# Working each normalization of a two-block network in two parts of 256 tokens, with the slab of matmuls ahead of it and the group behind it taken part by part

## The chip, the cores and the metric

The kernel runs on one core of one Trainium2 chip. The metric is the device time of one execution in microseconds (us), lower is better. The core has engines that each run their own instruction stream in order and meet through semaphores: TensorE (PE in the profile; PEld is its loading of weights), VectorE (DVE), ScalarE (ACT), GpSimd (POOL), and SyncE (SP), which here only issues the transfers of weights.

## The reference, cut to what is computed

Two blocks of a transformer run one behind the other, each of two layers, on 256 latent tokens and 256 context tokens with 1024 features, all in float32. Every layer normalizes its tokens, modulates them with a shift and a scale that come from a product of a conditioning vector with a weight, multiplies them with wide weights and adds the result, times a gate, to the residual. The latent and the context tokens have tables of their own.

```python
def rms_norm(x, gain=None):
    xf = x.astype(jnp.float32)
    y = xf * lax.rsqrt(jnp.mean(xf * xf, axis=-1, keepdims=True) + EPS)
...
def modulate(h, shift, scale):
    return h * (1.0 + scale) + shift

def swiglu(h, w_in, w_out):
    gate, up = jnp.split(h @ w_in, 2, axis=-1)
    return (jax.nn.silu(gate) * up) @ w_out
...
    for l in range(DEPTH):
...
        m_lat = (silu_c @ w_mod[l] + b_mod[l]).reshape(Bsz, N_MOD, 1, D)
...
        x = x + 0.5 * m_lat[:, 2] * swiglu(modulate(rms_norm(x), m_lat[:, 0], m_lat[:, 1]), ffn_in[l, 0], ffn_out[l, 0])
...
        h_lat = modulate(rms_norm(x), m_lat[:, 3], m_lat[:, 4])
...
        x = x + m_lat[:, 5] * o_lat
        x = x + 0.5 * m_lat[:, 8] * swiglu(modulate(rms_norm(x), m_lat[:, 6], m_lat[:, 7]), ffn_in[l, 1], ffn_out[l, 1])
```

The first block has attention with a recurrent branch in its layer 0 and windowed attention in layer 1. The second block has, in each layer, a mixer of three branches and a feed-forward part with a short convolution, with the same kind of normalization and modulation in front of each.

## The kernel before

**Layout.** All activations are held with features on the 128 partitions: a tensor is 8 tiles of 128 features ("k-tiles") by 512 tokens, the 256 latent ones first, the 256 context ones behind them (`HALVES` holds the two ranges, `NT` is 512, `KD` is 8). `X` is the residual. `H` holds the normalized and modulated tokens, `HH` their rounded high part and `HL` the rest. Weights are taken apart the same way, so every product is three matmuls: high by high, high by low, low by high. All outputs of a group stand in PSUM banks, one bank of 512 columns for each 128 output features.

**Slabs.** Weights arrive in slabs of 1 MB (4 k-tiles by 512 output columns, so 4 x 4 x 3 = 48 matmuls; in the deep product 2 k-tiles by 1024, also 48). SyncE loads them into a ring of three buffers (`slab_in`, issued at L2036): a slab's transfer waits until the slab that was three earlier has been used up. A slab is *split* into its high part by ScalarE (L1197, recorded at L1189, `WR<-ring`) and then its low part by VectorE (recorded at L1486, `WR<-ring,WR`), into one of two pairs of buffers, so ScalarE's write waits for TensorE to be done with the slab two earlier.

**Normalizations.** There are 12: `nf00`, `ne`, `n2`, `nf10`, `no`, `n11` and `fin` in the first block, `nm0`, `nc0`, `nm1`, `nc1` and `gfin` in the second. `n11`, `nc1`, `fin` and `gfin` cover 256 tokens, the others 512. One goes in this order, over all its tokens at once: ScalarE squares each tile of X as soon as its last addition is made (`sq`); TensorE adds the squares over the features in two steps of four tiles (`sum`, the second behind tile 7); ScalarE copies the sums out, TensorE turns them to one column for 128 tokens (`rstd`), VectorE and ScalarE form the reciprocal root, TensorE spreads it over the partitions (`spread`). Then for each of the 8 k-tiles VectorE multiplies (`times`, `H<-X,bank`), ScalarE modulates, one instruction for each half of tokens (`mod_h`, `H<-H,MOD`), and for even tiles also writes the high part; VectorE writes it for odd tiles and subtracts the low part for all (`mod_l`, `HL<-H,HH`).

**Products.** `lin` makes a product with 8 k-tiles in groups of four outputs, two slabs a group. A group is usually taken output by output. Its first group behind a normalization is taken k-tile by k-tile (`slab_all`), so that it can start at the first low part. `lin_deep` is the product out of a feed-forward part: 22 k-tiles, 8 outputs, 11 slabs. Where a product ends a layer part, its last slab is followed, output by output, by the addition of the bank into X (`ev`, L1495, for 512 tokens one instruction for each half) and by the square.

**Modulation tables.** The tables are products of one column with a weight as large as a layer. Their slabs of 1 MB (`in_w_mod`, `in_w_ada`) go through the same ring, but are used unsplit: eight matmuls of 512 columns on them (`bank<-ring,silc`). They run as background work in the loops over slabs of certain feed-forward parts: `between()` is called behind every slab and lets through, at a rate, so many steps of a generator (1.5 a slab in `f00`, 1.9 in `2`, 1.3 in `f10` and `c0`); what is left over runs behind the loop, ahead of the deep product.

**What sets the order.** The program first makes one list, `ORDER`, by calling these functions; then each engine's program walks it and issues its own part. The splits are put in last, in the loop at L780 to L795: ahead of each slab those of all slabs up to one further on, and one at each `split_next`, which stands behind the low part of k-tile 4 of a normalization:

```python
            if step[0] == "slab_all" or step[0] == "slab" and step[3] == 0:
                n = SLABS[step[1].slabs[step[2]][0]]["n"]
                while todo and SLABS[todo[0]]["n"] <= n + 1 and SLABS[todo[0]]["split_from"] <= at_hold:
                    steps.append(("split", todo.pop(0)))
```

In the profile many instructions bear the line of a helper: matmuls L820, ScalarE's activations L1189, VectorE's operations of two tensors L1486, with a scalar L1490 and L1492, additions with a gate L1495, reciprocals L1501.

## Time and profile before

| | |
|---|---|
| median of 3 runs | 4165.21 us (4158.31 to 4174.64) |
| profiled execution | 4163.52 us |
| its span in the trace | 4161.7 us |
| TensorE matmuls busy | 3745.4 us, 90% of the span |
| VectorE, ScalarE, GpSimd busy | 47%, 33%, 2% |
| mean granted clock of TensorE | 0.938 of full |
| transfers | 453.74 MB, mean 109 GB/s |

TensorE is busy for nine tenths of the span, though "busy" holds overlaps: consecutive matmuls of the same kind are pipelined and their ends are modelled, so counts and starts tell more than the sum of busy times. The other engines are idle more than half of the time. The span is that of one profiled execution; the 1.8 us between it and the execution's time lie around it.

### The profile page before, as it was taken

How to read it: one execution, taken by the hardware profiler on the slowest of the kernel's cores; microseconds unless marked ns; L12 is line 12 of the kernel's file. 1: busy time of each engine (PE TensorE's matmuls, PEld its weight loads, DVE VectorE, ACT ScalarE, POOL GpSimd, SP SyncE). 2: the span in 40 equal slices, each digit the busy share in tenths (PEclk: the TensorE clock that was granted, in tenths of full speed). 3: DMA queues.
4: the chain of work that ended last, by engine and by line, in shares of the span. 5: the costliest groups of instructions: out<-in, count | busy, mean ns of one | idle time of the engine just before them, and what ended most of it. 6: DMA issues, size and time to landing. Idle time of an engine off the chain costs nothing.

```text
span 4161.7 us, 59269 instructions
## 1 busy us (share of the span) xinstructions
PE 3745.4 (90%) x25936; PEld 2992.4 (72%) x25936; DVE 1969.7 (47%) x3272; ACT 1369.4 (33%) x2089; POOL 75.1 (2%) x106
## 2 busy tenths in 40 slices
PE   7999978588869999999989997998999999998898
PEld 4778754587646777677765996666777778777898
DVE  2223365888852223323355553654434453464575
ACT  3113324233331122222233443333233232343453
POOL 0000001100000000000000000010000000010000
PEclk9999988799989999999975998999999999999999
DMA  6553212000025552454220552121224442222453
GB/s 248 207 192 112 71 33 18 4 3 3 3 81 212 201 191 93 143 180 162 91 71 10 163 182 91 52 66 46 72 91 152 161 166 98 91 86 81 145 165 122
DMA packets 257906, 453.74 MB, mean 109 GB/s; under 512 B 14096, under 2 KB 157584, under 8 KB 243184
## 3 DMA queue, kind: packets, MB, share of 16 engines
q1 hardware_dynamic: 253840, 441.68, 31.2%
q0 software_dynamic: 3808, 8.27, 1.2%
q8 instruction: 204, 3.34, 0.3%
q14 instruction: 54, 0.44, 0.0%
HBM read 447.24 MB, written 1.94 MB: 108 GB/s over the span
## 4 chain that ended last, share of the span: by engine, by line
PE 73%; DVE 15%; ACT 7%; DMA 3%; issue 1%; POOL 0%; SPq 0%; DVEq 0%; ACTq 0%; POOLq 0%
PE bank L820 71%; DVE WR L1486 3%; ACT WR L1189 2%; DMA ring<-in_ffn_in 2%; ACT W L1189 2%; PE bank L991 2%; DVE W L1495 2%; DVE HF L1486 2%; DVE W L1501 1%; DVE W L1486 1%; DVE HF L1495 1%; ACT H L1189 1%; DVE H L1486 1%; DVE X L1495 1%; ACT HH L1189 1%
## 5 line engine op out<-in xcount | busy, mean ns | idle before, releaser
L820 PE MATMUL bank<-HH,WR 128*128 128x512 f32 (+1 forms) x8736 | 2401.0, 360 | 124.1 <-DVE WR L1486 71.9
L820 PEld LDWEIGHTS bank<-HH,WR 128*128 128x128 f32 x8736 | 1576.8, 193 | 436.5 <-issue 70.4
L820 PE MATMUL bank<-HL,WR 128*128 128x512 f32 (+1 forms) x4368 | 1558.1, 357 | 0.0
L1486 DVE TENSOR_TENSOR WR<-ring,WR 128x2048 fp32r<-128x2048 f32 (+2 forms) x300 | 675.5, 2252 | 1460.9 <-ACT WR L1189 1460.8
L1189 ACT ACTIVATE WR<-ring 128x2048 fp32r<-128x2048 f32 (+2 forms) x300 | 564.3, 1881 | 1450.9 <-PE bank L820 723.6
L820 PEld LDWEIGHTS bank<-HL,WR 128*128 128x128 f32 x4368 | 844.4, 193 | 109.9 <-issue 0.7
L820 PE MATMUL bank<-W 128*64 128x128 f32 (+5 forms) x1440 | 311.7, 374 | 29.8 <-DMA W<-W 10.4
L820 PEld LDWEIGHTS bank<-W 128*64 128x64 f32 (+3 forms) x1440 | 176.8, 173 | 93.8 <-issue 73.1
L1189 ACT ACTIVATE W<-bank 128x512 f32<-128x512 f32 (+3 forms) x371 | 180.0, 494 | 193.1 <-PE bank L820 171.7
L1189 ACT ACTIVATE W<-bank,small 128x512 f32<-128x512 f32 (+2 forms) x175 | 108.4, 619 | 355.7 <-DVE small L1490 246.3
L1495 DVE SCALAR_TENSOR_TENSOR W<-bank,vec,W 128x510 f32<-128x510 f32 (+1 forms) x206 | 130.3, 634 | 76.8 <-ACT W L1189 72.8
L820 PE MATMUL bank<-cst,W 64*64 64x64 f32 (+5 forms) x736 | 95.9, 283 | 71.7 <-POOL W L1989 30.8
L820 PE MATMUL bank<-ring,silc 128*32 128x512 f32 x960 | 133.6, 624 | 22.6 <-DMA ring<-in_w_mod 15.9
L820 PEld LDWEIGHTS bank<-cst,W 128*128 128x128 f32 (+2 forms) x736 | 80.6, 181 | 101.2 <-issue 47.1
L820 PE MATMUL bank<-HF 64*64 64x64 f32 x2816 | 110.2, 232 | 30.7 <-DVE HF L1495 21.8
L991 PEld LDWEIGHTS bank<-cst,W 128*128 128x128 f32 x432 | 53.4, 162 | 116.3 <-issue 53.4
L1713 DVE TENSOR_REDUCE small<-bank 128x1 f32<-128x512 f32 (+2 forms) x160 | 95.3, 595 | 80.2 <-PE bank L820 77.6
L820 PEld LDWEIGHTS bank<-HF 64*64 64x64 f32 x2816 | 99.0, 145 | 38.5 <-DVE HF L1495 25.0
L820 PE MATMUL bank<-W,cst 128*32 128x512 f32 (+3 forms) x304 | 72.2, 567 | 59.6 <-ACT W L1189 38.1
L1189 ACT ACTIVATE HF<-bank 64x256 f32<-64x256 f32 x160 | 60.4, 378 | 170.1 <-PE bank L820 158.2
L991 PE MATMUL bank<-cst,W 128*128 128x128 f32 x432 | 91.1, 331 | 24.7 <-DVE W L1490 18.2
L1189 ACT ACTIVATE W<-bank,vec 128x512 f32<-128x512 f32 (+1 forms) x144 | 88.1, 633 | 65.6 <-PE bank L820 64.6
(111 smaller groups left out, 2690.9 us busy)
## 6 DMA issues: line engine op xcount, KB each, us to landing
ring<-in_ffn_in SPq DMA_DIRECT2D x176, 512.0 KB, 5.3
ring<-in_w_mod SPq DMA_DIRECT2D x72, 1024.0 KB, 5.9
ring<-in_w_in SPq DMA_DIRECT2D x52, 1024.0 KB, 5.1
ring<-in_w_ada SPq DMA_DIRECT2D x48, 1024.0 KB, 7.0
ring<-in_ffn_out SPq DMA_DIRECT2D x176, 256.0 KB, 3.9
ring<-in_w_up SPq DMA_DIRECT2D x88, 512.0 KB, 5.0
ring<-in_w_down SPq DMA_DIRECT2D x88, 256.0 KB, 3.5
ring<-in_even_w_in SPq DMA_DIRECT2D x8, 1024.0 KB, 5.1
```

What stands on the lines that cost most here:

```text
L820: return e.matmul(o, l, r, start=start, stop=stop, skip_group_check=True)
L991: x = e.transpose(o[:, c * P:(c + 1) * P], a["P"][(i - 2) % 3][0][:, c * P:(c + 1) * P], C("ident"))
L1189: return e.activation(o, i, f, **kw).then_inc(ACTS.sem, ACTS.mark(*events))
L1486: put(e.tensor_tensor(o, a, b, op), *events)
L1495: put(e.scalar_tensor_tensor(out=o, in0=a, scalar=s, in1=b, op0=op0, op1=op1), *events)
L1501: put(e.reciprocal(o, a), *events)
L1713: put(e.tensor_reduce(neg, bank[:, lo:nk], AXX, ALU.max))
```

## The change

The tokens of a normalization are worked in two parts, 0 to 255 and 256 to 511. Every step that had a number of tokens now has a part `h`: squares, sums, reciprocal roots, spreads, multiplications, modulations and low parts. So for 512 tokens there are twice as many of each, half as wide.

- `last_slab`: the last slab of an addition into X (of 512 tokens) is run for all its outputs on part 0 (`slab_h`, `ev_h`), then for all its outputs on part 1. The sums, roots and spread of part 0 stand between the outputs of part 1, and the first two multiplications and modulations ahead of its last two additions.
- `first_group`: the first group behind a normalization is run k-tile by k-tile on part 0 (`slab_k`), with the sums, roots and spread of part 1 in between; then, if the group covers 512 tokens, on part 1: by k-tile in the first slab, by output in the second (`slab_h`). If the group covers only the 256 latent tokens (`no`, `nm1`), its outputs are copied out first and the rest of part 1 is prepared behind them.
- The low-part step `split_next` of `modnorm` is gone; the splits are put in by the loop over `ORDER`, ahead of a `slab_h` and of the first k-tile of each slab in `slab_k`, one slab further on, or none further on where both parts are taken and it is the second slab or part 1.
- `between()` isn't called for the first group any more, so the background steps that it let through run behind the loop.
- In the opening the eight multiplications of `nf00` no longer stand ahead of the modulation table but in `first_group`, and a `warm` step stands behind the first slab.
- The sums, roots and spreads (`norm`, `tok`, `bcast`) take one bank for each part.

The diff, cut:

```diff
                     last = k0 + kc == K
-                    if J.ready and J.ready[0] == "n" and g == 0:
-                        ORDER.append(("slab_all", J, len(J.slabs) - 1))
+                    if J.ready in SHIFTS and g == 0 and grouped.setdefault(J.ready, J) is J:
                         if last:
-                            for m in range(len(cols)):
-                                ORDER.append(("ev", J, g, m))
-                        if between:
-                            between()
+                            first_group(J)
+                        continue
+                    if last and g == len(groups) - 1 and kind == "add" and ntok == NT:
+                        last_slab(J, len(J.slabs) - 1, 4 * g)
                         continue
...
                             ORDER.append(("ev", J, g, m))
                             if kind == "add":
-                                square(kw["norm"], 4 * g + m, ntok)
+                                for h in range(ntok // 256):
+                                    square(kw["norm"], 4 * g + m, h)
...
+                if k0 + 2 == KF and ntok == NT:
+                    last_slab(J, len(J.slabs) - 1, 0)
+                    continue
...
+        def square(name, k, h, of=True):
+
+            ORDER.append(("sq", name, k, h, of))
+            if k == 5 and not (of and h == 0 and NORM_TOK[name] == NT):
+                ORDER.append(("sum", name, 0, h))
+            squared[name, h] = k + 1
...
+        def chunk_steps(name, k, h, last):
+
+            if k < KD:
+                ORDER.append(("times", name, k, h))
+                ORDER.append(("mod_h", name, k, h, *SHIFTS[name]))
+            if k > 0:
+                ORDER.append(("mod_l", name, k - 1, h, last))
+            chunked[name, h] = k + 1
...
+        def last_slab(J, i, c0):
+
+            name = J.kw["norm"]
+            s, g, k0, kc = J.slabs[i]
+            n = len(J.groups[g])
+            for m in range(n):
+                ORDER.append(("slab_h", J, i, m, 0))
+                ORDER.append(("ev_h", J, g, m, 0))
+                square(name, c0 + m, 0)
+            todo = [[("sum", name, 0, 0), ("sum", name, 1, 0)], [("rstd", name, 0)], [("spread", name, 0)]]
+            for m in range(n):
+                ORDER.append(("slab_h", J, i, m, 1))
+                if m >= n - 2:
+                    chunk_steps(name, m - n + 2, 0, False)
+                ORDER.append(("ev_h", J, g, m, 1))
+                square(name, c0 + m, 1)
+                if todo and (m + 1) % (n // 4) == 0:
+                    ORDER.extend(todo.pop(0))
+
+        def first_group(J):
+
+            name, K = J.ready, J.K
+            halves = 2 if NORM_TOK[name] == NT else 1
+            chunk = lambda k, h: chunk_steps(name, k, h, h == halves - 1) if k <= KD and chunked.get((name, h), 0) == k else None
+            both = J.ntok == NT
+            chunk(0, 0)
+            chunk(1, 0)
+            for k in range(K):
+                chunk(k + 2, 0)
+                ORDER.append(("slab_k", J, k // 4, k, 0))
+                if halves == 2:
+                    if name != "nf00":
+                        if k in (1, 3, 5):
+                            ORDER.append({1: ("sum", name, 1, 1), 3: ("rstd", name, 1), 5: ("spread", name, 1)}[k])
+                    if k >= 6:
+                        chunk(k - 6, 1)
+            if halves == 2:
+                if not both:
+                    for m in range(len(J.groups[0])):
+                        ORDER.append(("ev", J, 0, m))
+                for k in range(2, KD + 1):
+                    chunk(k, 1)
+            if both:
+                for k in range(4):
+                    ORDER.append(("slab_k", J, 0, k, 1))
+                for m in range(len(J.groups[0])):
+                    ORDER.append(("slab_h", J, 1, m, 1))
+                    ORDER.append(("ev", J, 0, m))
+            elif halves == 1:
+                for m in range(len(J.groups[0])):
+                    ORDER.append(("ev", J, 0, m))
...
         def modnorm(name, ntok, mod, i_shift, i_scale):
-            if name != "nf00":
-                norm(name, ntok)
-            for k in range(KD + 1):
-                if k < KD:
-                    if name != "nf00":
-                        ORDER.append(("times", name, k, ntok))
-                    ORDER.append(("mod_h", name, k, ntok, mod, i_shift, i_scale))
-                if k > 0:
-                    ORDER.append(("mod_l", name, k - 1, ntok))
-                if k == 5:
-                    ORDER.append(("split_next",))
+            assert SHIFTS[name] == (mod, i_shift) and NORM_TOK[name] == ntok
+            if name == "nf00":
+                return
+            if (name, 0) not in chunked:
+                norm(name, 0)
+                if ntok == NT:
...
+            ahead = None
+            if step[0] == "slab" and step[3] == 0:
+                ahead = 1
+            elif step[0] == "slab_h" and step[3] == 0:
+                ahead = 1
+            elif step[0] == "slab_k" and step[3] % 4 == 0:
+                both, n = step[1].ntok == NT, step[3] // 4
+                ahead = 0 if both and (n == 1 or step[4] == 1) else 1
+            if ahead is not None:
                 n = SLABS[step[1].slabs[step[2]][0]]["n"]
-                while todo and SLABS[todo[0]]["n"] <= n + 1 and SLABS[todo[0]]["split_from"] <= at_hold:
+                while todo and SLABS[todo[0]]["n"] <= n + ahead and SLABS[todo[0]]["split_from"] <= at_hold:
                     steps.append(("split", todo.pop(0)))
...
+            def slab_h(J, i, m, h):
 
                 s, g, k0, kc = J.slabs[i]
                 hi, lo = pair(s)
+                a, z = HALVES[h]
+                if m == 0:
+                    q.wait_ge(DVES, ("lo", s))
+                if h == 1 and J.kind in ("add", "deep"):
+                    q.wait_ge(DVES, ("x", J.kw["norm"], 4 * g + m, 0))
+                o = banks[BANK[J.name, g, m]][:, a:z]
+                for k in range(kc):
+                    if J.ready:
...
+                    mm(o, hi[:, w, n], ah[:, a:z], False, False)
+                    mm(o, hi[:, w, n], al[:, a:z], False, False)
+                    t = mm(o, lo[:, w, n], ah[:, a:z], False, last)
+                    if k == kc - 1:
+                        events = [(J.name, g, m, h)] if last else []
+                        if h == 1:
+                            events += [(J.name, g, m)] if last else []
+                            events += [("used", s)] if m == len(J.groups[g]) - 1 else []
+                        if events:
+                            t.then_inc(MM.sem, MM.mark(*events))
+                        if last and h == 1:
+                            shut((J.name, g, m))
...
+            def ev_h(J, g, m, h):
+                key = (J.name, g, m)
+                c, idx, (a, z) = 4 * g + m, J.kw["idx"], HALVES[h]
+                x = X[:, c, a:z]
+                q.wait_ge(MM, (*key, h))
+                stt(x, held(key)[:, a:z], MODS[J.kw["mod"]][:, idx * 8 + c, h:h + 1], x, ALU.mult, ALU.add,
+                    ("x", J.kw["norm"], c, h), *((("free", key),) if h else ()))
 
```

How it moves instructions is seen at two places. The first is VectorE at `ne`, the normalization behind `f00`, between its multiplications (`H<-X,bank`), high parts (`CAST`), low parts (`HL<-H,HH`) and the split of the second slab of the group behind (`WR<-ring1`). Before:

```order
L1486 TENSOR_TENSOR HL<-H,HH 128x512 [waits s_act_written]
L1486 TENSOR_TENSOR H<-X,bank6 128x512
L1498 CAST HH<-H 128x512 [waits s_act_written]
L1486 TENSOR_TENSOR HL<-H,HH 128x512 [waits s_dve_written]
L1486 TENSOR_TENSOR H<-X,bank6 128x512
L1486 TENSOR_TENSOR HL<-H,HH 128x512 [waits s_act_written]
L1486 TENSOR_TENSOR H<-X,bank6 128x512
L1498 CAST HH<-H 128x512 [waits s_act_written]
L1486 TENSOR_TENSOR HL<-H,HH 128x512 [waits s_dve_written]
L1486 TENSOR_TENSOR H<-X,bank6 128x512
L1486 TENSOR_TENSOR HL<-H,HH 128x512 [waits s_act_written]
L1486 TENSOR_TENSOR WR<-ring1,WR 128x2048 [waits s_act_written]
```

After (`X<-bank6` is the last addition of part 1; the two `small` operations belong to the next group):

```order
L1598 TENSOR_TENSOR H<-X,bank2 128x256
L1598 TENSOR_TENSOR HL<-H,HH 128x256 [waits s_act_written]
L1607 SCALAR_TENSOR_TENSOR X<-bank6,MOD0,X 128x256 [waits s_matmuls_done]
L1598 TENSOR_TENSOR small<-vec 128x15 [waits s_in_lam,s_in_sink,s_in_cst]
L1604 TENSOR_SCALAR small<-small 128x15 [waits s_dve_written]
L1598 TENSOR_TENSOR H<-X,bank2 128x256
L1610 CAST HH<-H 128x256 [waits s_act_written]
L1598 TENSOR_TENSOR HL<-H,HH 128x256 [waits s_dve_written]
L1598 TENSOR_TENSOR WR<-ring1,WR 128x2048 [waits s_act_written]
L1598 TENSOR_TENSOR H<-X,bank2 128x256
L1598 TENSOR_TENSOR HL<-H,HH 128x256
```

Before, the low parts 0 to 4 of 512 tokens stand ahead of the split; after, low parts 0 and 1 of 256 tokens do, and low part 2 stands behind it.

The second place is the end of the background work in `f00`, ahead of its deep product. On ScalarE, where `WR<-ring` is a split, `W<-bank` a gate of the feed-forward part or, at 64 partitions, the copy of a modulation row, and `HH<-W` the first high parts of the deep product, before:

```order
L1189 ACTIVATE WR<-ring0 128x2048 [waits s_matmuls_done,s_slab_landed0]
L1189 ACTIVATE W<-bank6 64x512 [waits s_matmuls_done]
L1189 ACTIVATE WR<-ring1 128x2048 [waits s_slab_landed1]
L1189 ACTIVATE W<-bank7 128x512 [waits s_dve_written,s_matmuls_done]
L1189 ACTIVATE W<-bank0 128x512 [waits s_dve_written,s_matmuls_done]
L1189 ACT_TABLE_LOAD
L1189 ACTIVATE small<-small 128x1
L1189 ACTIVATE HH<-W 128x512 [waits s_matmuls_done]
```

After:

```order
L1301 ACTIVATE WR<-ring0 128x2048 [waits s_slab_landed0]
L1301 ACTIVATE WR<-ring1 128x2048 [waits s_matmuls_done,s_slab_landed1]
L1301 ACTIVATE W<-bank1 128x512 [waits s_dve_written,s_matmuls_done]
L1301 ACTIVATE W<-bank2 128x512 [waits s_dve_written,s_matmuls_done]
L1301 ACTIVATE W<-bank5 64x512 [waits s_matmuls_done]
L1301 ACT_TABLE_LOAD
L1301 ACTIVATE small<-small 128x1
L1301 ACTIVATE HH<-W 128x512 x6
```

The second split stood behind the copy of the modulation row and needed only its transfer; now it stands ahead of the gates and the copy, and needs a release by TensorE as well. On SyncE, which loads the ring buffers, before:

```order
L2036 DMA ring1<-in_ffn_in 128x4x256 [waits s_dve_written]
L2036 DMA ring1<-in_ffn_in 128x4x256
L2036 DMA ring2<-in_w_mod 128x2x1024 [waits s_matmuls_done]
L2036 DMA ring0<-in_ffn_in 128x4x256 [waits s_matmuls_done]
L2036 DMA ring0<-in_ffn_in 128x4x256
L2036 DMA ring1<-in_ffn_out 128x512 [waits s_dve_written]
```

After:

```order
L2159 DMA ring0<-in_ffn_in 128x4x256 [waits s_matmuls_done]
L2159 DMA ring0<-in_ffn_in 128x4x256
L2159 DMA ring1<-in_w_mod 128x2x1024 [waits s_dve_written]
L2159 DMA ring2<-in_w_mod 128x2x1024 [waits s_matmuls_done]
L2159 DMA ring0<-in_w_mod 128x2x1024 [waits s_dve_written]
L2159 DMA ring1<-in_ffn_out 128x512 [waits s_matmuls_done]
```

Before, a slab of `in_ffn_in` was the last ahead of the deep product; now three modulation slabs in a row are, and the first slab of the deep product (`in_ffn_out`) goes to buffer 1 behind TensorE's use of one of them.

## Rows read from the trace of the kernel before

**Rows 1.** The page's chain that ended last, by engine.
```profile
PE 73%; DVE 15%; ACT 7%; DMA 3%; issue 1%; POOL 0%; SPq 0%; DVEq 0%; ACTq 0%; POOLq 0%
```

**Rows 2.** Timeline of TensorE at `ne`: start, length, instruction, count, idle before.
```profile
453.19 1.06 PE L820 MATMUL bank<-W,cst 128*32 128x512 f32 x8 [1.63 <-ACT W L1189]
...
463.04 0.79 PE L820 MATMUL bank<-HH,WR 128*128 128x512 f32 x1 [3.29 <-DVE HL L1486]
```

**Rows 3.** Stretches: length, busy (count) of five engines, granted clock, transfer share, GB/s.
```profile
2073.71:2083.73 10.02, 3.49 (x26) 2.10 (x25) 3.25 (x8) 4.31 (x9) 0.00 (x0) 0.82 0.01 2
3114.30:3125.81 11.51, 5.17 (x25) 3.72 (x24) 3.25 (x8) 3.93 (x8) 0.00 (x0) 0.65 0.00 1
```

**Rows 4.** Stretches from the last slab to the first group's end, six places.
```profile
439.09:487.70 48.61, 41.77 (x177) 32.63 (x176) 24.11 (x43) 22.76 (x36) 0.00 (x0) 0.86 0.06 17
1209.98:1260.35 50.37, 41.58 (x185) 31.27 (x183) 21.34 (x33) 22.32 (x33) 0.00 (x0) 0.90 0.19 63
1650.00:1700.69 50.69, 41.59 (x185) 31.28 (x183) 26.03 (x42) 25.07 (x37) 0.00 (x0) 0.90 0.18 63
2061.42:2102.92 41.50, 31.62 (x177) 26.79 (x176) 25.55 (x41) 23.12 (x36) 0.00 (x0) 0.84 0.12 39
3102.19:3153.38 51.19, 43.06 (x185) 32.56 (x183) 23.47 (x35) 22.12 (x32) 0.00 (x0) 0.87 0.18 62
3524.56:3567.27 42.71, 32.80 (x177) 27.92 (x175) 25.56 (x48) 24.62 (x38) 0.00 (x0) 0.80 0.15 50
```

**Rows 5.** Stretches without a wait of TensorE, 512 and 256 columns wide.
```profile
1180.00:1200.00 20.00, 20.00 (x89) 16.53 (x89) 5.53 (x9) 3.81 (x4) 0.00 (x0) 1.00 0.31 106
2450.00:2480.00 30.00, 30.00 (x252) 30.00 (x252) 16.02 (x18) 12.63 (x15) 0.00 (x0) 1.00 0.56 179
```

**Rows 6.** Groups by form, VectorE, 3920 to 3945 us: busy, mean ns | idle before.
```profile
L1486 DVE TENSOR_TENSOR WR<-ring,WR 128x2048 fp32r<-128x2048 f32 x3 | 6.9, 2291 | 6.9 <-ACT WR L1189 6.9
...
L1486 DVE TENSOR_TENSOR HL<-H,HH 128x256 fp32r<-128x256 f32 x6 | 2.6, 425 | 1.1 <-ACT HH L1189 0.8
L1495 DVE SCALAR_TENSOR_TENSOR X<-bank,MOD,X 128x256 f32<-128x256 f32 x4 | 1.8, 480 | 0.9 <-PE bank L820 0.9
```

**Rows 7.** Groups by form, ScalarE, 3920 to 3945 us.
```profile
L1189 ACT ACTIVATE H<-H,MOD 128x256 f32<-128x256 f32 x8 | 4.8, 598 | 4.8 <-DVE H L1486 4.8
```

**Rows 8.** Timeline of TensorE: two waits, before modulation matmuls and for a split.
```profile
1248.33 1.06 PE L820 MATMUL bank<-ring,silc 128*32 128x512 f32 x8 [2.44 <-ACT silc L1189]
...
2094.36 0.58 PE L820 MATMUL bank<-HH,WR 128*128 128x256 f32 x1 [3.22 <-DVE WR L1486]
```

**Rows 9.** Stretches just behind two waits for a split.
```profile
2094.30:2101.10 6.80, 6.74 (x33) 6.75 (x34) 5.62 (x9) 4.52 (x6) 0.00 (x0) 0.54 0.26 80
3909.60:3916.40 6.80, 6.72 (x44) 6.72 (x45) 3.68 (x5) 0.96 (x3) 0.00 (x0) 0.75 0.84 261
```

**Rows 10.** Timeline of VectorE in the opening.
```profile
33.83 4.87 DVE L1486 TENSOR_TENSOR H<-X,bank 128x512 f32<-128x512 f32 x8 [1.36 <-PE bank L820]
```

**Rows 11.** Timeline of all engines ahead of the deep product of layer `2`.
```profile
1521.97 16.60 SPq L2036 DMA_DIRECT2D ring<-in_ffn_out  x16
...
1529.02 1.92 ACT L1189 ACTIVATE WR<-ring 128x2048 fp32r<-128x2048 f32 x1 [11.79 <-DMA ring<-in_ffn_out]
1530.85 1.06 ACT L1189 ACTIVATE W<-bank 128x512 f32<-128x512 f32 x2
1532.96 1.91 PE L820 MATMUL bank<-ring,silc 128*32 128x512 f32 x8
1534.92 0.59 ACT L1189 ACTIVATE W<-bank 64x512 f32<-64x512 f32 x1 [3.01 <-PE bank L820]
1538.41 0.77 PE L820 MATMUL bank<-HH,WR 128*128 128x512 f32 x1 [1.80 <-DVE HL L1486]
```

**Rows 12.** Timeline of TensorE ahead of the deep product of `f00`.
```profile
326.07 0.39 PE L820 MATMUL bank<-HH,WR 128*128 128x512 f32 x1
...
328.60 0.47 PE L820 MATMUL bank<-HH,WR 128*128 128x512 f32 x1 [1.16 <-DVE HL L1486]
```

205 lines of the change are left out of this document (110 added, 95 removed).

## The prediction, made before the changed kernel had run

> **What bounds the kernel now.** I read the page's chain that ended last first: TensorE holds 73% of it, VectorE 15% and ScalarE 7%, so the end moves by what TensorE does or waits for [rows 1]. The next view is TensorE's own timeline over one normalization, `ne`, at 451 us: after the last matmul in front of it TensorE waits for the square, does a few small matmuls, waits again, and starts the next large product at 463.04, with the sum, transposition and spread of 512 tokens in between [rows 2]. The table of stretches shows such a pause at each of six places, 10.0 us at the shortest and 11.5 at one of the longest, with the granted clock at 0.82 and 0.65 of full there, a mean of its two levels of 1.2 and 2.4 GHz [rows 3]. These six are `ne`, `n2`, `nf10`, `no`, `nc0` and `nm1`.
>
> For a measure that also holds what comes just behind, I take each place from the start of the last slab in front to the end of the first group behind: 48.61, 50.37, 50.69, 41.50, 51.19 and 42.71 us [rows 4]. In clean stretches a matmul of 512 columns takes 20.00/88 = 0.227 us and one of 256 columns 30.00/250 = 0.120 us (the counts less the one or two that overlap the edges) [rows 5]. The places hold 144 such matmuls: 32.7 us where all are 512 wide, 22.4 us at `no` and `nm1`, whose first group has 256 tokens. `n2`, `nf10` and `nc0` also hold one slab of modulation matmuls (1.0 us). What is left is loss: 15.9, 16.7, 17.0, 19.1, 17.5 and 20.3 us, 106.5 us together, or 2.6% of the span. That is all that the change can win at the six.
>
> **What it adds in TensorE work.** A 512-wide matmul becomes two of 256: 2 x 0.120 - 0.227 = 0.013 us each. 144 are split at each of four places, 48 at `no` and `nm1` (last slab only), 96 at the opening and at `nm0`: 864, 11.2 us in all; the walk below holds it. The profile thus prices the second instruction at 13 ns. The Trainium skill (page TensorE: Matmul & The Clock Gate, section Back-to-back issue gap) gives N/2.4 plus 2.5 ns for an isolated matmul; by it the 864 would cost 2.2 us. The trace disagrees for this stream of alternating weight loads, and the measurement decides.
>
> **A walk through `ne` and `nf10` after the change.** Time 0 is the start of the last slab. Durations are the 256-wide ones of the normalization `nc1`, which has only 256 tokens: VectorE 0.42 for a multiplication or a low part, 0.48 for an addition into X [rows 6]; ScalarE 0.60 for a modulation [rows 7]. An addition in a row of several follows the last by 0.4. The small groups on TensorE take half of their 512-wide 1.06 us [rows 2]. Splitting a slab takes 1.9 us on ScalarE, then 2.3 on VectorE [rows 6, 11].
> - TensorE does the first 256 tokens of the slab until 5.8. VectorE is busy with a split until 4.2, so the eight additions end at 7.4 and the last square at 7.9. TensorE waits 0.7 for it, does two sums and goes on with the second part.
> - The copy of the sums stands on ScalarE behind the squares of the second part, which wait for additions that wait for TensorE: the second wait, 1.5 us. The reciprocal square root and spread of part one then hide behind the remaining slabs. TensorE ends the slab at 16.5 and waits 0.6 for the first low part: it starts the next group at 17.1, where it idled 11 us before.
> - It needs 1.44 us per k-tile. VectorE has low parts 0 and 1 ready at 17.1 and 18.5. Then, by the new order, comes the split of the group's second slab, which formerly stood behind low part 4 and now stands ahead of low part 2. ScalarE reaches it at 18.9, after the third modulation; 1.9 and 2.3 us later VectorE multiplies once more and gives low part 2 at 23.9. TensorE has been out of work since 20.6 (one sum included): **a wait of 3.3 us**. The nearest row is a split waited for 3.22 us at 2094 [rows 8]. Behind it k-tiles come every 0.9 us on VectorE and ScalarE, so TensorE is the slower; one wait of 0.3 at the second reciprocal is left. The group ends at 45.6.
>
> 45.6 less 32.7 is 12.9. To this comes the clock. Behind that wait at 2094 and behind a like one at 3909 the granted clock stands at 0.54 and 0.75 over the next 6.8 us [rows 9]; at half level half the time is lost, so 0.25 to 0.46 of 6.8, or 1.7 to 3.1 us. I take 2.5. Loss after: 15.4, against 15.9 and 17.0. At `n2` and `nc0` the slab has four larger outputs; the same walk has waits of 1.0 (copy of the sums), 0.6 and 3.5 us and ends 1.0 earlier: 14.4, against 16.7 and 17.5. The latter two and `nf10` also lose an old wait, 2.44 us at 1248, where the modulation matmuls wait for the new table's silu on ScalarE [rows 8]: the deferred first modulation slab takes it out, and it is in the losses before.
>
> At `no` only the first part is needed by the group, but its third split also stands in the stream, ahead of low part 6: a second wait of 3.3 us, the group ends at 37.2, loss 14.8 plus 5.0 for the clock at two waits. Then the next group needs the second part, whose modulations stood behind the group's four output copies (1.9 us), and its second slab's split stands behind all of them (2.5 us). Together 24.2, against 19.1. At `nm1` the next group is 512 wide and hides the last of these: 20.7, against 20.3 and 1.2 behind it. The six give -0.5, -1.6, -2.3, -3.1, +5.1 and -0.8: **-3.2 us**.
>
> **The other normalizations.** At the opening the first product starts some 2.4 us earlier, as eight 512-wide multiplications (4.87 us) no longer stand ahead of the modulation table [rows 10], but the wait at low part 2 (1 us) and 96 splits (1.3) use it up: 0. At `nm0`, where ScalarE takes all 16 squares ahead of the first modulation, the same: -0.5. At `n11` and `nc1` (256 tokens) the earlier split costs about 1 us each. Sum **+1.5 us**. `fin` and `gfin` stay.
>
> **The end of the layers ahead.** The first group no longer calls the background work of modulation tables, so the slabs that it took come at the end of the loop. In `f00` the SP queue has the first slab of the deep product in the ring buffer of a modulation slab that TensorE uses only behind the last input slab, and ScalarE has its split ahead of that slab's gates. From the start of the last input slab: matmuls until 10.9, first modulation slab until 12.6 (1.7 us each by the row of 1.91 for eight, less the overlap [rows 11]). Then the transfer starts. At the end of layer `2` a split began 7.05 us behind such an issue, with another slab's transfer in front of it [rows 11]; here none is in front, and I take 6.0 (between 5 and 7.05): 18.6. Split 1.9, gates 1.1, then 3.5 from the copy of the modulation row to the first deep product [rows 11]: 25.1. Before it was 10.9 and the 2.4 us from the end of the last matmul's slot (326.07 + 0.2) to 328.60 [rows 12], 13.3, plus 5.1 for three moved slabs: +6.6, and 2.0 for the clock. In layer `2` with four slabs behind and one in front of the transfer: 14.3 + 7.0 + 1.9 + 1.1 + 3.5 = 27.8, against 16.5 (1521.97 to 1538.41) [rows 11] + 5.1: +6.2 and 1.7. `f10` and `c0` have their buffer free in time: +1 and -1. Sum **+16.5 us**.
>
> **Total.** The profiled execution took 4163.5 us, of which 4161.7 is the span and 1.8 lies around it: 4163.5 - 3.2 + 1.5 + 16.5 = 4178.3. The median is 1.7 above that execution, so 4180 for the median. Waits gained at the front of each group are paid back at its second slab and at two layer ends.
>
> **Rivals.**
> - *The parts overlap as meant.* If ScalarE and VectorE reach the split without holding up low part 2, each of the six keeps 1.9 for split matmuls, 4.4 for small groups and 2.8 of short waits, 9.1: 106.5 - 54.6 = 52 gained, and with +18 from the rest 4131. For it: VectorE is busy only 24 of the 48.6 us of `ne` [rows 4]. Against it: both queues work in order, and the split stands in them where the new order says. Chance 0.14.
> - *Layer ends and the ring decide for slower.* From 2 us more per transfer at the four ends (2 x 4 = 8), and the clock losing 3.1 in place of 2.5 at eight waits (+5), the time is 4193. For it: the clock already stands at a mean of 0.65 in the pause of `nc0` [rows 3]. Against it: two of the four ends have a free buffer. Chance 0.20.
> - *Short waits cost no clock.* If the 3.3 us waits leave the clock at full, eight times 2.5 less: 4160. Chance 0.14. The change doing nothing is the same band.
>
> **Chances.** My forecast has 0.52 (its own range 4168 to 4192, a fifth of it above 4186). About 0.5%, 21 us, is what a measurement of this kernel can tell from no change. Faster: the first rival, less its nearer half-outcomes, 0.12. Slower: 0.18 of the second and 0.10 of the forecast, 0.28. Within 0.5%: 0.60. The range reaches down to 4148, two thirds of the way to the first rival, and up to 4198, the second rival with 5 us for a third late buffer.
>
> **What would show it.** In the profile after: TensorE's start of each next group within 1 us of the last slab's end; a wait of some 3 us "<- DVE HL" or "<- DVE WR" 3.5 us behind it at each place, with the WR subtraction just ahead on VectorE; two waits of 5 us or more at the ends of `f00` and `2`, ScalarE waiting there for `in_ffn_out`; no wait for `silc` over 1 us. If the 3 us waits are absent I was wrong on the order's effect, and the kernel is faster; if the layer ends run on, the transfer's timing was wrong.

## The result, and the profile after

The changed kernel takes 4189.83 us in the median of 10 runs (4183.77 to 4361.37), the kernel before 4173.3 us (4158.31 to 4252.7). The ratio is 1.0052, with a 95% interval of 1.0035 to 1.0068: slower, by about 22 us. Two further comparisons of the same pair of kernels gave 1.0048 (1.0031 to 1.0065) and 1.0067 (1.0051 to 1.0084), so by the ratios the size lies between 20 and 28 us; the plain medians differ by 16.5, 17.7 and 26.4. The forecast was 4180, 15 us over the kernel before. Its range held the result, but it had given a slowdown of more than 0.5% a chance of 0.28, and no change within 0.5% one of 0.60: what happened lies just beyond that border.

The profile that came with the first timing was of an execution at a mean granted clock of 0.841 all through, 4% longer than the others, so it is not read here. What follows is from two later profiled executions of the same kernel, `e1_after` (4186.69 us) and `e1b_after` (4191.16 us).

The page of `e1_after`: the span, then busy time, share and instructions of each engine, then the chain that ended last by engine.

```profile
span 4184.9 us, 61559 instructions
...
PE 3756.1 (90%) x26928; PEld 3039.6 (73%) x26928; DVE 1989.1 (48%) x3448; ACT 1398.2 (33%) x2206; POOL 75.1 (2%) x106
...
PE 72%; DVE 16%; ACT 7%; DMA 4%; issue 1%; POOL 0%; SPq 0%; DVEq 0%; ACTq 0%; POOLq 0%
```

TensorE issues 992 instructions more (the 864 split matmuls, and the small groups in two parts), and its share of the chain is 72%, against 73% before [rows 1]. So the page as a whole tells almost nothing: what was gained and what was lost lie in different stretches.

**The six places.** These are the stretches of `e1_after` from the start of the last slab to the end of the first group, in the order of [rows 4] and with the columns of [rows 3]:

```profile
445.64:494.62 48.98, 42.81 (x337) 39.82 (x336) 26.99 (x65) 25.94 (x50) 0.00 (x0) 0.93 0.06 17
1225.31:1269.47 44.16, 39.61 (x338) 37.28 (x336) 25.69 (x56) 24.68 (x42) 0.00 (x0) 1.00 0.16 50
1666.86:1713.92 47.06, 41.35 (x337) 38.36 (x336) 28.93 (x64) 27.75 (x50) 0.00 (x0) 0.96 0.15 48
2077.83:2115.32 37.49, 28.61 (x242) 25.90 (x240) 22.36 (x47) 20.63 (x39) 0.00 (x0) 1.00 0.17 57
3120.66:3164.70 44.04, 39.62 (x338) 37.30 (x336) 26.23 (x57) 24.14 (x41) 0.00 (x0) 1.00 0.16 50
3542.33:3586.27 43.94, 33.01 (x242) 30.11 (x240) 24.55 (x57) 24.32 (x44) 0.00 (x0) 0.88 0.22 73
```

The pause of some 11 us is gone everywhere, and yet `ne` takes 48.98 us where it took 48.61. TensorE's own timeline there shows what stands in its place; of the start-by-start list these are all entries with a wait of more than 0.25 us.

```profile
453.72 1.07 PE L900 MATMUL bank<-W,cst 128*32 128x256 f32 x16 [0.73 <-DVE X L1607]
...
457.81 0.58 PE L900 MATMUL bank<-cst,W 128*128 128x1 f32 x4 [1.39 <-ACT W L1301]
...
465.15 0.36 PE L900 MATMUL bank<-HH,WR 128*128 128x256 f32 x1 [1.11 <-DVE small L1598]
...
471.63 0.38 PE L900 MATMUL bank<-HH,WR 128*128 128x256 f32 x1 [2.81 <-DVE HL L1598]
```

The prediction's walk through `ne` had these four waits as 0.7, 1.5, 0.6 and 3.3 us; they are 0.73, 1.39, 1.11 and 2.81. The first matmul of the next group starts 1.11 us behind the last slab, where 11 us lay before [rows 2]. The last wait is made as the walk said, which VectorE's timeline shows:

```profile
465.85 0.43 DVE L1598 TENSOR_TENSOR HL<-H,HH 128x256 fp32r<-128x256 f32 x1
468.62 2.29 DVE L1598 TENSOR_TENSOR WR<-ring,WR 128x2048 fp32r<-128x2048 f32 x1 [2.34 <-ACT WR L1301]
470.82 0.41 DVE L1598 TENSOR_TENSOR H<-X,bank 128x256 f32<-128x256 f32 x1
471.16 0.42 DVE L1598 TENSOR_TENSOR HL<-H,HH 128x256 fp32r<-128x256 f32 x1
```

Low part 1 ends at 466.28. Then VectorE waits 2.34 us for ScalarE's half of the split, splits for 2.29, and only then comes to low part 2, for which TensorE has been waiting.

**The end of `f00`.** SyncE, ScalarE and TensorE ahead of its deep product in `e1_after`:

```profile
320.25 5.34 PE L900 MATMUL bank<-ring,silc 128*32 128x512 f32 x24
322.21 11.97 SPq L2159 DMA_DIRECT2D ring<-in_ffn_out  x16
328.17 1.91 ACT L1301 ACTIVATE WR<-ring 128x2048 fp32r<-128x2048 f32 x1 [26.22 <-DMA ring<-in_ffn_out]
329.98 1.54 ACT L1301 ACTIVATE W<-bank 128x512 f32<-128x512 f32 x3
331.53 1.28 ACT L1301 ACT_TABLE_LOAD   x1
331.57 1.87 PE L900 MATMUL bank<-cst,W 64*128 64x4 f32 x8 [5.97 <-ACT W L1301]
```

The transfer is issued when the first of three modulation slabs in a row has been used, its split begins 5.96 us later (the forecast took 6.0), and the gates, the copy and all behind them stand behind that split. TensorE waits 5.97 us. The deep product starts at 334.62, 25.5 us after the last input slab's start at 309.11; the forecast had 25.1, and before it was 13.3 [rows 12].

### The profile page after: what moved, and what is told of

Its sections match the earlier page's. It is cut to its first block, busy times and chain, and to the rows that moved or that the text cites. A ratio compares the mean times of both kernels' runs of the same rounds, so it can differ in the third digit from the quotient of the medians.

```text
span 4359.6 us, 61559 instructions
## 1 busy us (share of the span) xinstructions
PE 3953.4 (91%) x26928; PEld 3107.9 (71%) x26928; DVE 1991.6 (46%) x3448; ACT 1400.4 (32%) x2206; POOL 74.9 (2%) x106
## 4 chain that ended last, share of the span: by engine, by line
PE 75%; DVE 14%; ACT 6%; DMA 3%; issue 1%; POOL 0%; SPq 0%; DVEq 0%; ACTq 0%; POOLq 0%
PE bank L900 73%; DVE WR L1598 3%; ACT WR L1301 2%; ACT W L1301 2%; PE bank L1103 2%; DVE W L1607 2%; DVE W L1613 1%; DVE W L1598 1%; DMA ring<-in_ffn_in 1%; DVE HF L1598 1%; DVE HF L1607 1%; DVE X L1607 1%; DVE ring L1598 1%; DVE H L1598 0%; DVE HL L1598 0%
## 5 line engine op out<-in xcount | busy, mean ns | idle before, releaser
L900 PE MATMUL bank<-HH,WR 128*128 128x512 f32 (+1 forms) x9312 | 2542.0, 360 | 125.3 <-DVE HL L1598 59.0
L900 PEld LDWEIGHTS bank<-HH,WR 128*128 128x128 f32 x9312 | 1682.5, 197 | 483.1 <-issue 74.5
L900 PE MATMUL bank<-HL,WR 128*128 128x512 f32 (+1 forms) x4656 | 1663.4, 357 | 0.0
L900 PEld LDWEIGHTS bank<-HL,WR 128*128 128x128 f32 x4656 | 918.7, 197 | 130.5 <-issue 0.9
L900 PE MATMUL bank<-W 128*64 128x128 f32 (+5 forms) x1440 | 330.0, 390 | 28.5 <-DMA W<-W 10.3
L900 PE MATMUL bank<-ring,silc 128*32 128x512 f32 x960 | 146.6, 681 | 16.7 <-DMA ring<-in_w_mod 16.7
L900 PE MATMUL bank<-HF 64*64 64x64 f32 x2816 | 115.4, 239 | 27.2 <-DVE HF L1607 20.5
L900 PE MATMUL bank<-W,cst 128*32 128x256 f32 (+2 forms) x432 | 78.5, 473 | 48.4 <-ACT W L1301 26.1
L1103 PE MATMUL bank<-cst,W 128*128 128x128 f32 x432 | 94.2, 340 | 23.2 <-DVE W L1602 17.7
L1301 ACT ACTIVATE H<-H,MOD 128x256 f32<-128x256 f32 x144 | 86.5, 601 | 78.6 <-DVE H L1598 77.7
```

Of the source, the lines that this page charges most:

```text
L900: return e.matmul(o, l, r, start=start, stop=stop, skip_group_check=True)
L1103: x = e.transpose(o[:, c * P:(c + 1) * P], a["P"][(i - 2) % 3][0][:, c * P:(c + 1) * P], C("ident"))
L1301: return e.activation(o, i, f, **kw).then_inc(ACTS.sem, ACTS.mark(*events))
```

## How the kernels were compared stretch by stretch

The columns of all large matmuls add up to 5,529,600 in every kernel here, so "the moment at which so many columns have been issued" is the same point of the work in each, however the matmuls are cut. The table gives how much later than in the kernel before each stretch ends, as the change over that stretch, in us; the forecast's terms are put on the same stretches (place and layer end together, since the moved modulation slabs cross the border between them).

| stretch | forecast | `e1_after` | `e1b_after` | before with deferral alone, `e5_before_defer` |
|---|---|---|---|---|
| opening and `f00` | +8.6 | +6.6 | +10.1 | +6.7 |
| `ne`, last slab and first group | -0.5 | +0.4 | +0.3 | -1.5 |
| even mixer | 0 | +8.4 | -0.1 | -1.4 |
| `n2` and layer `2` | +5.6 | +1.5 | +0.8 | +0.9 |
| `nf10` and `f10` | -0.6 | -0.5 | +1.4 | -1.5 |
| `no` and odd mixer | +5.1 | +0.9 | +3.3 | -0.9 |
| `n11` and its layer part | +1 | +2.6 | +4.0 | -0.7 |
| `nm0` | -0.5 | +1.5 | +3.1 | +0.3 |
| mixer of the second block | 0 | -2.9 | -1.8 | -3.0 |
| `nc0` and `c0` | -4.1 | -0.7 | +0.7 | +2.7 |
| `nm1` and mixer | -0.8 | -0.8 | -0.6 | +2.3 |
| `nc1` and what follows | +1 | +6.1 | +6.3 | +1.0 |
| sum | +14.8 | +23.1 | +27.6 | +5.1 |

A difference of a few us need not be one between kernels: single executions differ too. The even mixer's +8.4 is the plainest case. Between the same two waits the granted clock was 0.85 in `e1_after`, 0.92 in `e1b_after` and 0.93 before:

```profile
637.63:720.77 83.14, 79.20 (x352) 45.53 (x353) 47.17 (x160) 36.57 (x99) 2.15 (x3) 0.85 0.01 3
```
```profile
639.92:716.25 76.33, 72.39 (x353) 41.95 (x353) 47.00 (x160) 36.57 (x99) 2.15 (x3) 0.92 0.01 4
```
```profile
629.31:705.53 76.22, 72.28 (x352) 41.89 (x353) 47.01 (x160) 36.51 (x99) 2.14 (x3) 0.93 0.01 3
```

The work is the same; the clock came back to full later in one execution. The second execution was run to ask just this, and it shows that the 8.4 us don't belong to the kernel: they come and go between executions of one program. Why the clock comes back late in some is not shown. So the stretches tell where something happens, and the medians of several runs how much it is worth.

## Experiments

**The kernel again.** No edit.

> The changed kernel as it is, for a profile and for a time beside the others. Theory (the prediction's): 10 to 27 us over the kernel before, with a wait of TensorE for a low part about 3.5 us behind the start of each first group, 2 to 3.5 us long, and waits of 5 us or more ahead of the deep products of f00 and 2. Rival (the parts overlap as meant and the loss is elsewhere): no wait over 1 us at the third k-tile of the first groups, and the groups end some 9 us earlier each, so that the layer ends would have to lose over 60 us.

Measured: 4185.06 against 4167.41, ratio 1.0048 (1.0031 to 1.0065). The wait is at the third k-tile, and the ends of `f00` and layer `2` wait 5.97 and 5.18 us. The theory holds.

> The changed kernel once more, for a second profile. In the first one the stretch of the even mixer between ne and n2 took 8.4 us more than before with the same waits, at a granted clock that came back to full some 20 us later. Theory (the clock's return depends on what the program did just ahead, so it belongs to the kernel): the stretch takes 728 to 732 us again and the granted clock is 0.79 or lower 60 to 80 us behind n2's far end of the first attention. Rival (chance of one execution): the stretch takes 720 to 723 us as in the other kernels.

Measured: 4191.96 against 4165.54, ratio 1.0067 (1.0051 to 1.0084). The even mixer took 722.2 us: the theory that the late return of the clock belongs to the kernel fell, the rival holds.

**The split later.**

```diff
             elif step[0] == "slab_k" and step[3] % 4 == 0:
-                both, n = step[1].ntok == NT, step[3] // 4
-                ahead = 0 if both and (n == 1 or step[4] == 1) else 1
+                ahead = 0
+            elif step[0] == "slab_k" and step[3] == 2 and step[4] == 0:
+                ahead = 1
+            elif step[0] == "slab_k" and step[3] == 6 and step[1].ntok != NT:
+                ahead = 1
```

> The changed kernel with the split of a first group's second slab put in ahead of k-tile 2 of the group (behind low part 3) in place of ahead of k-tile 0 (behind low part 1), and at the groups of 256 tokens the third slab's ahead of k-tile 6 in place of 4. The work is the same. Theory (the wait at low part 2 is made by the split's place): the wait of 2.5 to 3.3 us goes and one of at most 0.7 us at k-tile 4 comes; with 1 to 2.5 us of clock given back at some ten places, 25 to 50 us under the changed kernel. Rival (VectorE and ScalarE have no room for the split before k-tile 4 wherever it stands): the wait only moves to k-tile 4, and the time is within 8 us of the changed kernel.

Measured: 4166.24 us, 18.8 under the changed kernel beside it, ratio to the kernel before 0.9995 (0.9984 to 1.0006). It lies between the two expectations, and the trace says why. The wait for low part 2 is gone, but at `ne` TensorE now has this one, at k-tile 3 of the group:

```profile
465.47 0.36 PE L903 MATMUL bank<-HH,WR 128*128 128x256 f32 x1 [1.11 <-DVE small L1601]
...
474.39 0.61 PE L903 MATMUL bank<-cst,W 128*128 128x1 f32 x4 [2.19 <-ACT W L1304]
```

It is the root of part 1, which needs ScalarE's copy of the sums, and that stands behind the split now. So at the four places whose group has 512 tokens only 0.4 to 0.8 us were won in this pair of traces. The gain is where the group has 256 tokens: `nm1` 5.3 us, `nc1` 4.6, `n11` 3.1. There the third slab's split stood in the group too. The two waits that it and the second made at `nc1` (1.06 and 2.18 us in `e1_after`) are gone, and `nc1` took 27.24 us, against 26.95 before and 31.80 in the changed kernel. These three explain some 13 of the 18.8 us. At `no`, whose group has 256 tokens too, nothing was won (37.44 us against 37.49): its waits are 1.6 us shorter, but the clock was 0.95 where it had been 1.00. The rest can't be read from this pair of traces, since 8.8 us of their difference are the even mixer's, which is chance (`e3_background` and `e4_both`, below, are the cleaner pair).

**The background work back inside the loops.** The rates 1.5, 1.9 and 1.3 become 1.65, 2.0 and 1.43:

```diff
-        ffn("f00", A["ffn_in"][0, 0], A["ffn_out"][0, 0], 0, NT, 0, "ne", (cols["m0"], 1.5))
+        ffn("f00", A["ffn_in"][0, 0], A["ffn_out"][0, 0], 0, NT, 0, "ne", (cols["m0"], 1.65))
...
-        ffn("2", A["ffn_in"][0, 1], A["ffn_out"][0, 1], 6, NT, 0, "nf10", (cols["m1"], 1.9))
-        ffn("f10", A["ffn_in"][1, 0], A["ffn_out"][1, 0], 0, NT, 1, "no", (cols["a0"], 1.3))
+        ffn("2", A["ffn_in"][0, 1], A["ffn_out"][0, 1], 6, NT, 0, "nf10", (cols["m1"], 2.0))
+        ffn("f10", A["ffn_in"][1, 0], A["ffn_out"][1, 0], 0, NT, 1, "no", (cols["a0"], 1.43))
```

> The changed kernel with the rates of the background modulation work raised (1.5 to 1.65, 1.9 to 2.0, 1.3 to 1.43), so that as many modulation slabs run inside the loops as in the kernel before, although the first group calls none. Theory (the layer ends cost 16.5 us since the modulation slabs are left over): the waits ahead of the deep products of f00, f10 and c0 go back to those of before, and that of 2 at least in part: 8 to 18 us under the changed kernel. Rival (the ends only look longer, the loss is in the first groups): within 3 us of the changed kernel.

Measured: 4166.96 us, 18.1 under the changed kernel, ratio to before 0.9998 (0.9987 to 1.0008). All four ends are as short as before, or nearly. From the last input slab to the deep product's second slab, layer `2` took 41.8 us in `e1_after` and 31.8 here, `f10` 29.1 and 23.7, `c0` 36.0 and 27.6; before they were 30.2, 23.7 and 27.6. At the end of `2`:

```profile
1538.55 1.05 PE L900 MATMUL bank<-cst,W 64*128 64x4 f32 x8 [0.69 <-ACT W L1301]
1541.40 0.77 PE L900 MATMUL bank<-HH,WR 128*128 128x512 f32 x1 [1.80 <-DVE HL L1598]
```

These ends also held the moved work: in `f10` and `c0` 24 matmuls more than before, two modulation slabs and the turning of one row. So the loops must be counted with them. Loop and end together, `2` is 9.1 us shorter than in `e1_after`, `f10` 2.8, `c0` 12.8. In `f00` nothing was won: its end is as before (25.9 us), but its loop took 257.1 us in place of 241.9 (246.5 before), with a new wait for a split in the middle:

```profile
177.27 0.79 PE L900 MATMUL bank<-HH,WR 128*128 128x512 f32 x1 [8.06 <-DVE WR L1598]
```

Nor is all of the gain in `c0` a loss taken back. TensorE had one long wait in its loop, for ScalarE's copy of a modulation row, in the kernel before and in the changed one:

```profile
3308.64 1.68 PE L820 MATMUL bank<-cst,W 128*128 128x8 f32 x8 [4.57 <-ACT W L1189]
```
```profile
3342.90 1.88 PE L900 MATMUL bank<-cst,W 128*128 128x8 f32 x8 [4.73 <-ACT W L1301]
```

With the raised rate it is gone; the loop took 239.3 us, against 243.8 and, in the kernel before, 244.6. So by an estimate from these traces some 4 to 5 of the 18.1 us are an old wait that the other order of slabs took out, and some 13 are the change's own loss.

**The deferral alone, in the kernel before.** The first group no longer calls the background work; nothing is worked in parts. The order of all transfers is then that of the changed kernel.

```diff
                             for m in range(len(cols)):
                                 ORDER.append(("ev", J, g, m))
-                        if between:
-                            between()
                         continue
```

> The kernel before, with one part of the change alone: the first group no longer calls the background work, so the order of all transfers is that of the changed kernel; all 512 tokens are still normalized at once. Theory: +16.5 us at the ends of the layers, less three waits of 2.4 us for the silu of the new table that go with the deferral: 6 to 14 us over the kernel before. Rival (the ends hide it): within 3 us of before, or under it by the three waits, 7 us.

Measured: 4172.57 against 4167.41 us, ratio 1.0016 (1.0007 to 1.0025): 5 to 7 us, at or just under the lower end of the theory's 6 to 14. It has two sides. The places `n2`, `nc0` and `nf10` gain 5.5, 5.4 and 4.9 us, as the modulation slabs and the wait for `silc` leave them, and the first group of `f00` 3.0; from there to the last slab of the deep product `f00` loses 9.3 us, `2` 6.4, `f10` 3.5 and `c0` 8.0. Set against each other, `f00` loses 6.3, `2` 0.9 and `c0` 2.6, and `f10` gains 1.4. That is also why `e3_background` can win more than the deferral costs: it keeps the gains at the places and takes back the losses at the ends. Beside it in the same comparison the changed kernel took 4185.06, so of its 18 us there the deferral makes 5 and the work in two parts 12.5. The forecast had these at 9 (16.5 less three waits of 2.44) and 6.

**Both remedies.** The edits of `e2_late_split` and `e3_background` together.

> The changed kernel with the late split and the raised rates of the background work together. Theory (two causes at separate places, and each gave 18 us alone): 20 to 36 us under the changed kernel, so 4 to 16 us under the kernel before. Rival (both runs gained the same thing, the clock of the even mixer, and it can be gained only once): within 5 us of the kernel before.

Measured: 4144.5 against 4165.54 us, ratio 0.9950 (0.9936 to 0.9965). That is 21 us under the kernel before, where the theory had 4 to 16, and 47 under the changed one beside it (four runs), where it had 20 to 36. The two gains of 18.8 and 18.1 add up, and rather more: counted through the kernel before, the sum is 38.7 (21.0 and the 17.7 of `e1_after`'s comparison). The rival, that both had gained the same thing, fell. But the 21 us under the kernel before are not all the work of the two parts: the old wait of 4.6 us in `c0` is among them. Against `e3_background`, which differs by the split's place alone, the stretches of `ne`, `n2`, `nf10`, `no`, `n11`, `nc0`, `nm1` and `nc1` sum to 313.6 us where they were 334.7: 21 us, 2 at a place of 512 tokens, 3 to 4.5 at `n11`, `nc1` and `no`, 1 at `nm1`. This version beats both kernels.

**Root and spread of part 1 later.** On top of `e4_both`:

```diff
-                        if k in (1, 3, 5):
-                            ORDER.append({1: ("sum", name, 1, 1), 3: ("rstd", name, 1), 5: ("spread", name, 1)}[k])
+                        if k in (1, 4, 6):
+                            ORDER.append({1: ("sum", name, 1, 1), 4: ("rstd", name, 1), 6: ("spread", name, 1)}[k])
```

> As the run with late split and raised rates, and the root and the spread of part 1 stand behind k-tiles 4 and 6 of the first group in place of 3 and 5, since with the late split TensorE waited 1.8 to 2.3 us at k-tile 3 for ScalarE's copy of the sums, which stood behind the split. Theory (the wait comes from the order on ScalarE): the wait goes at ne, n2, nf10, no, nc0 and nm1, at most 0.5 us comes ahead of part 1; 6 to 12 us under the run without it. Rival (ScalarE and VectorE have no room): the wait moves to k-tile 4 or to part 1, within 3 us.

Measured: 4145.22 us, no change (4144.5 without it). The wait for the copy is gone and two for low parts have come:

```profile
476.51 0.35 PE L903 MATMUL bank<-HH,WR 128*128 128x256 f32 x1 [1.71 <-DVE HL L1601]
...
484.24 0.39 PE L903 MATMUL bank<-HH,WR 128*128 128x256 f32 x1 [0.63 <-DVE HL L1601]
```

1.71 and 0.63 in place of 2.20. The rival holds. With the split ahead of low part 2 the wait is 2.8 us, with it later 2.2, with root and spread later too 1.7 and 0.6: in none of the three orders tried do ScalarE and VectorE have it done ahead of k-tile 4 without TensorE waiting. That no order could is not shown.

**One call of the background work in `f00`.** On top of `e6_steps`, with the old rate:

```diff
                             first_group(J)
+                            if between and J.ready == "nf00":
+                                between()
                         continue
```

> As the run before it, but in f00 the old rate of 1.5 and one call of the background work behind the first group. With the raised rate f00 had one wait of 8.06 us for a split behind two modulation slabs, and no wait at its end. Theory (that wait comes from the order of the slabs in the ring): it goes and the end stays without a wait of 5 us: 5 to 10 us under the run with the raised rate. Rival (transfers bound the loop of f00, so the wait comes elsewhere in it): within 3 us.

Measured: 4145.4 us, no change (4145.22 without it). `f00` from its first group to the deep product's second slab took 283.8 us against 282.3: 3 us less in the loop, 4.4 more at the end. The rival holds as far as `f00` goes: modulation slabs that leave one end of it turn up as a wait at another place.

**The copy of the sums first.** On top of `e4_both`, in `last_slab`:

```diff
-                ORDER.append(("ev_h", J, g, m, 1))
-                square(name, c0 + m, 1)
-                if todo and (m + 1) % (n // 4) == 0:
-                    ORDER.extend(todo.pop(0))
+                step = todo.pop(0) if todo and (m + 1) % (n // 4) == 0 else []
+                if step and step[0][0] == "rstd":
+                    ORDER.extend(step)
+                ORDER.append(("ev_h", J, g, m, 1))
+                square(name, c0 + m, 1)
+                if step and step[0][0] != "rstd":
+                    ORDER.extend(step)
```

> As the run with late split and raised rates, with one step moved in the last slab: ScalarE's copy of the sums of part 0 (and the root behind it) stands ahead of the second square of part 1, not behind it. TensorE waited 1.39 us there at ne, nf10, no and nm1 and 0.86 us at n2 and nc0. Theory (the prediction's walk: the copy stands behind squares that wait for additions that wait for TensorE): these six waits fall under 0.4 us, 4 to 8 us under the run without it. Rival (what is saved is waited for at the start of the next group, since that waits for low part 0 behind the last additions): the wait at the group's start grows by as much, within 2 us.

Measured: 4142.4 us against 4144.5, ratio to before 0.9950 (0.9933 to 0.9966): too little to tell from no change. The wait fell from 1.39 to 0.68 us, half of what was expected, and the others stayed as they were:

```profile
459.66 0.58 PE L906 MATMUL bank<-cst,W 128*128 128x1 f32 x4 [0.68 <-ACT W L1307]
...
465.67 0.36 PE L906 MATMUL bank<-HH,WR 128*128 128x256 f32 x1 [1.12 <-DVE small L1604]
```

So what was saved was not waited for at the group's start, as the rival would have it. `n2` and `nf10` are 1.0 and 2.0 us shorter than in `e4_both`, `ne` 0.7 longer, at a lower clock; the six places together took 252.5 us, against 258.5. The time is the rival's, the mechanism is not, and what became of the saved time stays open between the single traces and the noise of the medians.

**The price of a split matmul.** In the kernel before, 1488 matmuls of `f10`:

```diff
-                    mm(o, *terms[0], first, False)
-                    mm(o, *terms[1], False, False)
-                    t = mm(o, *terms[2], False, last)
+                    if J.name in ("f10i", "f10o"):
+                        for z in (0, 256):
+                            q_, r_ = o[:, z:z + 256], (r[0][:, z:z + 256], r[1][:, z:z + 256])
+                            mm(q_, l[0], r_[0], first and z == 0, False)
+                            mm(q_, l[0], r_[1], False, False)
+                            t = mm(q_, l[1], r_[0], False, last and z == 256)
+                    else:
+                        mm(o, *terms[0], first, False)
+                        mm(o, *terms[1], False, False)
+                        t = mm(o, *terms[2], False, last)
```

> The kernel before, with 1488 of the 512-wide matmuls of the feed-forward part f10 (all groups but the first, and the deep product) issued as two of 256 columns each, in the same places; nothing else is changed. Theory (the rows of 0.227 and 0.120 us: 13 ns for a second instruction): 19 us over the kernel before, all of it in f10. Rival (the time of the columns alone counts and a second instruction costs 2 to 3 ns, as in the Trainium skill, page TensorE: Matmul & The Clock Gate, section Back-to-back issue gap): 3 to 5 us over it.

Measured: 4178.52 against 4165.06 us, ratio 1.0034 (1.0022 to 1.0047), 9 to 20 us. In the trace nine slabs of the deep product, all but the first and the last, 432 such matmuls without a wait in either kernel, took 103.68 us against 97.92: 13.3 ns for each. In the same stretch 250 of 256 columns take 30 us, as in [rows 5]:

```profile
2000.00:2030.00 30.00, 30.00 (x252) 30.00 (x251) 7.38 (x7) 8.24 (x8) 0.00 (x0) 1.00 0.28 90
```

The profile's price holds. The Trainium skill (page TensorE: Matmul & The Clock Gate, section Back-to-back issue gap) has 2.5 ns for each further matmul in its formula for an isolated one, so an estimate of 1.1 us for these 432; the measurement is 5.76 us, and it decides. From the loop, 9.8 us came for 912 of them, 10.8 ns each. Two waits for a split there, 1.1 us together in the kernel before, are gone, which accounts for half of the 2.4 us that are missing to 13.3 ns each.

**The old rate in `f00`.** `e8_copy_first` with 1.65 put back to 1.5 in `f00`.

> As the run with the moved copy, with the rate of the background work in f00 back at 1.5. With 1.65 the stretch of f00 from its first group's end to the deep product's second slab took 284 us, with 1.5 in the changed kernel 280.5, in the kernel before 272.4. Theory (the two add up over separate stretches): 3 to 4 us under the run with 1.65. Rival (the wait at the end of f00 comes out longer behind the late split): within 2 us.

Measured: 4140.0 against 4165.06 us, ratio 0.9933 (0.9919 to 0.9948), 2.4 us under `e8_copy_first`, in the direction of the theory but within the noise. In the traces the stretch of `f00` is 280.6 us against 284.1, as expected. It is the fastest kernel of this study, 25 us under the kernel before.

**The deep product's split out of the way, in `f00`.** On top of `e10_f00_rate`:

```diff
             if step[0] == "slab" and step[3] == 0:
-                ahead = 1
+                ahead = 0 if step[1].name == "f00i" and step[2] == 21 else 1
```

> As the run with the moved copy and the rate of 1.5 in f00, with the split of the deep product's first slab taken out from ahead of f00's last input slab: it now stands behind the gates, the copy of the modulation row and the first high parts, so these no longer wait on ScalarE for the transfer of in_ffn_out. Theory (the end of f00 is a chain of transfer, split, gates, copy and high parts on one queue, and the split can lie beside the rest): the stretch from f00's last input slab to the deep product's second slab falls from 38.6 to 33 to 36 us. Rival (the transfer and the two halves of the split are the whole chain, whatever stands beside it): 38 us or more, since the low parts of the slab now end later.

Measured: 4140.9 us, no change; the end of `f00` took 38.40 us against 38.64. The transfer was issued 13.1 us behind the start of the last input slab, as in `e1_after`. The wait for the copy fell to 0.69 us, and the wait for the split grew to 7.71:

```profile
325.66 1.05 PE L906 MATMUL bank<-cst,W 64*128 64x4 f32 x8 [0.69 <-ACT W L1307]
334.42 0.79 PE L906 MATMUL bank<-HH,WR 128*128 128x512 f32 x1 [7.71 <-DVE WR L1604]
```

The rival holds: moving the split on ScalarE changed nothing. What is left is the chain from the transfer, which waits for the ring, through the two halves of the split. No run frees the ring earlier with all else the same.

## Why the prediction was right, and where it was not

The direction and most of the mechanism hold: waits gained at the front of each group are paid back at its second slab and at the ends of the layers. The later split gives 18.8 us back. The background work inside the loops gives back 18.1, of which some 13 were the change's. The size (15 us forecast, 20 to 28 by the ratios) is of the right order, with several terms off.

- **Price of the split matmuls.** 13 ns forecast, 13.3 measured in `e9_halved`.
- **The walk through `ne`.** Waits of 0.7, 1.5, 0.6 and 3.3 us forecast, 0.73, 1.39, 1.11 and 2.81 measured. The rest of the loss, split matmuls and small groups, was 1.9 + 4.4 = 6.3; it is 48.98 - 32.7 less 6.0 of waits and 3.4 for the clock (7% of 48.98), 6.8. At `n2`, `nf10`, `no` and `nc0` the wait at low part 2 was 2.44 or 2.45 us in `e1_after`, where the walk had 3.3 and 3.5.
- **The clock at short waits: mis-sized.** The forecast took 2.5 us a wait at every place. The granted clock is 1.00 over the whole of `n2`, `no` and `nc0` in `e1_after`, so nothing was lost there; it is 0.93, 0.96 and 0.88 at `ne`, `nf10` and `nm1`. Over the six, one less the clock times the length, an estimate of what the lower clock cost, is 10.6 us in `e1_after` and 16.2 in `e1b_after`, where eight times 2.5 were forecast. The rival "short waits cost no clock" was half right. The two rows it was sized from [rows 9] were of places where it did fall.
- **The losses at the six.** 15.4, 14.4, 15.4, 19.8, 14.4 and 20.7 forecast, with 4.4 more behind `no`. Measured in `e1_after` 16.3, 11.5, 14.4, 15.1, 11.3 and 21.5, and 4.9 behind `no`. The sum of 104.5 is 95.0, and 100.2 in `e1b_after`: 9.5 and 4.3 us less, close to the 9.4 and 3.8 by which the clock was put too high. At `no` and `nm1` the second wait came as said, 3.07 and 3.08 us.
- **The end of `f00` and of `2`.** 25.1 and 27.8 us from the last input slab to the deep product forecast, 25.5 and 28.1 measured. The steps are right too: from the transfer's issue to the split 6.0 and 7.0 us forecast, 5.96 and 6.90 measured.
- **The end of `c0`: the step that failed.** `f10` and `c0` "have their buffer free in time: +1 and -1". The transfer of the deep product's first slab was issued 11.6 us ahead of the last input slab in the kernel before; in `e1_after` it is issued 0.5 us behind that slab's start in both layers. So the premise was wrong for both. The price was wrong only in `c0`. In `f10` the wait hides behind two modulation slabs that now stand there: TensorE waits 0.72 and 1.79 us where it waited 1.54, and the layer came out 1.1 and 1.4 us above the forecast in the two traces. In `c0` the gates go back and forth between ScalarE and VectorE for 9.3 us behind the late split (1.1 us on ScalarE alone in `f10`), and TensorE waits 6.01 and 2.64 us where it waited 3.86. The layer is 6.5 us above the forecast in both traces; the stretch in the table shows less, since `nc0` in front of it lost 3.1 and 1.6 us less than forecast. This is the end of `c0`:

```profile
3408.52 0.34 SPq L2159 DMA_DIRECT2D ring<-in_w_ada  x1
3408.91 29.98 SPq L2159 DMA_DIRECT2D ring<-in_w_down  x20
3416.41 1.92 ACT L1301 ACTIVATE WR<-ring 128x2048 fp32r<-128x2048 f32 x1 [12.18 <-DMA ring<-in_w_down]
3427.53 1.88 PE L900 MATMUL bank<-cst,W 128*128 128x8 f32 x8 [6.01 <-ACT W L1301]
3432.05 0.77 PE L900 MATMUL bank<-HH,WR 128*128 128x512 f32 x1 [2.64 <-DVE HL L1598]
```

- **`n11` and `nc1`: mis-sized.** About 1 us each was taken for the earlier split; they lost 2.6 to 4.1 and 4.9 us. A group of 256 tokens holds not only its second slab's split but the third's, as the forecast itself had it at `no`. With both later (`e2_late_split`) they are back at 27.2 us.
- **`nm0` and `no`.** `nm0` lost 1.5 to 3.1 us where -0.5 was forecast. In `e1_after` its waits of more than 0.4 us add up to 21.4 us, as before (21.5), so the earlier start that was to pay for the 96 split matmuls (1.3 us) didn't come; the rest differs between the two executions. `no` lost less than forecast, mostly by the clock.

The errors went both ways. Less was lost than forecast at `n2` with layer `2` (4 to 5 us) and at `no` (2 to 4), more at `c0` with `nc0` (3 to 5), behind `n11` and `nc1` (7 to 8 together) and at `nm0` (2 to 4). That the total came out nearer than its terms is luck.

**The rivals.** "The parts overlap as meant" had the six places lose 54.6 us. With the split out of the way (`e2_late_split`) they lose 82.7, against 106.5 before and 90.1 in `e1_after`, since a wait of some 2 us stays at the third k-tile and the clock is under 1.00 at four of them. "Layer ends and the ring decide for slower" had 4193, which is nearer to the measured 4190 than the forecast, but not for its reasons: the transfers at the ends of `f00` and `2` took what the forecast had, the clock cost less and not more, and only `c0` bears it out. "Short waits cost no clock" holds for `n2`, `no` and `nc0` in one of two executions.

## What to carry to other kernels

Working in parts takes away a pause only if every step that stood inside the pause finds a place beside the new overlap; here the split of the next slab had filled the pause for nothing, and cost TensorE a wait of 2.4 to 3 us at each as soon as there was none. Background work that is put off isn't free work later: at the end of a loop its transfers block a ring that the next stage needs, so look at what is issued behind it, on every in-order queue. When a remedy wins more than the loss that it was meant for, look for an old wait that went with it; the loop of `c0` had one. And where a remedy moves a wait on and makes it hardly shorter, as twice here, ask whether the engines have room at all before the next deadline.

## What the runs showed of the chip

The granted clock doesn't fall at each short wait: with waits of 0.86, 1.12 and 2.44 us in 44 us it stayed at 1.00 at `n2` in `e1_after`, and the same place with the same waits had 0.96 in `e1b_after`. And behind the same long pause in the even mixer the same work took 83.14 us at a mean clock of 0.85 in one execution and 76.33 at 0.92 in another, with nothing changed in the program. `e12_end_split`, whose mixer is the same code, took 83.08 us for that work too, at 0.85. Such steps of 2 to 8 us in single executions are as large as the effects looked for here.
